# Attention in one streaming encoder layer: negated scores with a chained minimum, a fourth slot for turned weights, the output gate on GpSimd, stores on SyncE

## What is computed

```python
def dsa_attend(q, iq, iw, k, v, ik, q_pos, topk):
    ...                                             # sel: the topk keys that the indexer picks for a query
    logits = jnp.einsum('btgrd,btkgd->btgrk', qg, kg).astype(jnp.float32) * (A_HEAD_DIM ** -0.5)
    logits = logits - slopes[None, None, :, :, None] * dist[:, :, None, None, :]
    logits = jnp.where(valid[:, :, None, None, :], logits, -jnp.inf)
    prob = jax.nn.softmax(logits, axis=-1).astype(v.dtype)
    out = jnp.einsum('btgrk,btkgd->btgrd', prob, vg)
    return out.reshape(bsz, t, A_WIDTH)
# later: y_a = (o_a * silu(z_a)) @ w_branch_a
```

## Time and profile before

| | us |
|---|---|
| median of 3 runs | 3327.56 |
| lowest, highest | 3320.19, 3329.63 |
| the profiled execution, its time | 3322.89 |
| its span in the trace | 3321.2 |
| attention in the trace, first S to the store of the last tile | 1840.66 to 2523.75 |
| TensorE, VectorE, ScalarE, GpSimd busy in 1842 to 2525 | 559, 538, 402, 105 |

### The profile page before, as it was taken

One profiled execution on the slowest core, in us unless ns is written; L12 is line 12 of the kernel. 1 busy time (PEld: TensorE's weight loads), 2 busy tenths in 40 slices (PEclk: granted clock), 3 DMA queues, 4 the chain that ended last, 5 costly groups with the idle time before them and its releaser, 6 DMA issues.

```text
span 3321.2 us, 43027 instructions
## 1 busy us (share of the span) xinstructions
PE 2869.1 (86%) x14677; PEld 2570.8 (77%) x14677; DVE 2374.1 (71%) x4343; ACT 1601.6 (48%) x2638; POOL 1260.8 (38%) x875
## 2 busy tenths in 40 slices
PE   5899999999999989898642678888886999599998
PEld 4899999999999989898631455666665999488886
DVE  5378758629999999999346777878776646456564
ACT  3277477877776857656002555556653000211111
POOL 1000377777788768576040321111102333111120
PEclk9999999999999999999886899999998999799999
DMA  4333333333333223222483121111104455311210
GB/s 139 91 118 125 111 102 103 97 115 105 107 112 100 93 77 113 70 88 93 160 222 100 43 58 43 44 48 32 41 11 157 139 180 199 132 62 62 80 64 32
DMA packets 286182, 321.04 MB, mean 97 GB/s; under 512 B 37025, under 2 KB 258977, under 8 KB 282413
## 3 DMA queue, kind: packets, MB, share of 16 engines
q1 hardware_dynamic: 149037, 176.64, 17.7%
q10 hardware_dynamic: 135648, 137.80, 12.5%
q0 software_dynamic: 1312, 4.26, 0.4%
HBM read 194.46 MB, written 123.48 MB: 96 GB/s over the span
## 4 chain that ended last, share of the span: by engine, by line
PE 41%; DVE 36%; ACT 8%; issue 7%; DMA 4%; POOL 2%; ACTq 1%; SPq 0%; DVEq 0%; POOLq 0%
PE psum L2054 12%; DVE s_high L427 10%; PE psum L1177 10%; PE psum L1929 7%; DVE a_l L1760 4%; ACT s_ajunk L410 3%; DVE a_ptlo L1779 3%; PE psum L1663 2%; ACT v_product L820 2%; PE psum L1699 2%; DVE s_cand L429 2%; DVE s_g L428 1%; DVE s_high L459 1%; PE psum L1700 1%; PE psum L1157 1%
## 5 line engine op out<-in xcount | busy, mean ns | idle before, releaser
L1177 PE MATMUL psum<-hT_hi,j_whi 128*128 128x416 f32 x2440 | 870.8, 357 | 69.4 <-ACT j_out L1050 32.6
L1177 PE MATMUL psum<-hT_hi,j_wlo 128*128 128x416 f32 x2440 | 862.5, 353 | 0.0
L1177 PE MATMUL psum<-hT_lo,j_whi 128*128 128x416 f32 x2440 | 862.1, 353 | 0.0
L834 POOL TENSOR_TENSOR v_y<-v_y,v_product 128x422 f32<-128x422 f32 x580 | 712.9, 1265 | 256.2 <-ACT v_product L820 256.0
L1177 PEld LDWEIGHTS psum<-hT_hi,j_whi 128*128 128x128 f32 x2440 | 463.6, 190 | 87.7 <-ACT j_out L1050 39.1
L1177 PEld LDWEIGHTS psum<-hT_lo,j_whi 128*128 128x128 f32 x2440 | 464.7, 190 | 11.6
L1177 PEld LDWEIGHTS psum<-hT_hi,j_wlo 128*128 128x128 f32 x2440 | 463.6, 190 | 6.1
L427 DVE TENSOR_SCALAR_CACHE_REDUCE s_high<-s_key,s_cand 128x1024 int16<-128x1024 f32 (+4 forms) x240 | 392.9, 1637 | 8.4
L820 ACT ACTIVATE v_product<-v_x,v_taps 128x422 f32<-128x422 f32 x580 | 339.6, 640 | 74.7 <-POOL v_y L834 34.5
L1779 DVE TENSOR_TENSOR a_ptlo<-psum,a_pthi 128x512 fp32r<-128x512 f32 x338 | 228.2, 684 | 55.6 <-ACT a_pthi L1735 54.9
L1728 ACT ACTIVATE a_l<-a_l,a_nbias 128x512 f32<-128x512 f32 (+4 forms) x136 | 184.2, 1354 | 167.0 <-DVE a_nbias L1769 165.7
(11 more groups left out here) (286 smaller groups left out, 5401.3 us busy)
## 6 DMA issues: line engine op xcount, KB each, us to landing
T_dram<-j_out ACTq DMA_DIRECT2D x305, 208.0 KB, 1.9
j_w<-in_w_in ACTq DMA_DIRECT2D x59, 512.0 KB, 4.2
m_gate<-T_dram SPq DMA_DIRECT2D x60, 416.0 KB, 3.5
m_oraw<-B_dram SPq DMA_DIRECT2D x15, 832.0 KB, 6.5
SC_dram<-i_acc SPq DMA_DIRECT2D x40, 256.0 KB, 2.0
M_dram<-m_merged ACTq DMA_DIRECT2D x5, 1664.0 KB, 10.5
n_x<-in_x_prompt SPq DMA_DIRECT2D x16, 512.0 KB, 4.8
a_q<-T_dram SPq DMA_DIRECT2D x32, 256.0 KB, 6.6
```

The source lines that it names most:

```text
L834: pool.tensor_tensor(y[n % 2][:], y[n % 2][:], product[n % RING][:], ALU.add).then_inc(added, 1)
L1177: last = pe.matmul(bank, w[p][:, k, :], h[:, k, t0:t0 + SPAN], start=(k == 0 and q == 0), stop=(k == KD - 1 and q == 2))
```

## The change

The order of groups is the same; the program is written out tile by tile with constants. What differs:

- **Scores are negated**: the scale of the queries and of `nd` changes sign, R keeps the minimum, and takes as its start the minimum of the piece before (a value per partition, `lows[:, h, s-1:s]`), so the last piece holds the minimum of the head. E takes it as its bias, with scale -1. Before each R but a head's first, VectorE waits for its own R before it. L1768 and L1769 are gone.
- **A fourth slot** of turned weights takes the PSUM bank that the share had; the share now takes a turn in the ring, after W of the fourth last key tile. T runs up to 4 key tiles ahead: T of tile x+4 stands behind W of tile x, and T 2 and T 3 of a group stand before its first S.
- **The gate on GpSimd**: ScalarE copies the share to SBUF (`a_factor`, L1745 of the changed kernel) behind the last hi; GpSimd multiplies it by the gate (L1622), and later the added output by that (L1628). VectorE keeps the add alone.
- **Stores on SyncE**, each behind the loads of the tile two later.
- **Groups' ends** stand at x = 1 in place of x = 0.
- Loads of `nd` and of the gate wait for the last E and the last gate product, not for a tile's output.

```diff
-            pool.memset(scale[:, h:h + 1], HD ** -0.5 * 2.0 ** (h + 1)).then_inc(scale_set, 1)
+            pool.memset(scale[:, h:h + 1], -(HD ** -0.5) * 2.0 ** (h + 1)).then_inc(scale_set, 1)
...
-    QK, PT, PO, PB = 2, (2, 3, 4), (5, 6), 7
+    QK, PT, PO = 2, (2, 3, 4, 7), (5, 6)
...
-            if x == 0 and before:
+            if x == 1 and before:
                 e.finish(before)
...
+        def gate(group):
+            u, nu, _ = group.shares
+            pool.wait_ge(pt_free[u], nu + 1)
+            pool.wait_ge(za_full[group.p], group.m * 16 + 16)
+            pool.tensor_tensor(factor[group.g][:], factor[group.g][:], of_group(za, group), ALU.mult).then_inc(factor_made, 1)
+            pool.wait_ge(factor_made, group.n + 1)
+
+        def end(group):
+            o = of_group(oa, group)
+            pool.wait_ge(po_read[group.g], group.t + 1)
+            pool.tensor_tensor(o, o, factor[group.g][:], ALU.mult).then_inc(o_done[group.p], 1)
+
-        split(0, 0, 0)
-        with pool.Fori(0, DT // 2) as i:
-            split(i * 2 + 1, i, 1)
-            store(i * 2, i, 0)
-            split(i * 2 + 2, i + 1, 0)
-            store(i * 2 + 1, i, 1)
+        split(0)
+        split(1)
+        for group in groups:
+            if group.n:
+                end(groups[group.n - 1])
+            gate(group)
+            if group.g == 0 and 1 <= group.t < TILES - 1:
+                split(group.t + 1)
+        end(groups[-1])
...
+            if x + RING < tiles:
+                turn(group, x + RING)
+            if x + RING == tiles:
+                share(group)
+            if x + 2 >= tiles and following:
+                turn(following, x + 2 - tiles)
...
+            if s:
+                _, _, _, _, previous, uses, _ = group.units[(h - 4 * group.g) * len(pieces(group.keys)) + s - 1]
+                vec.wait_ge(qk_read[previous], uses + 1)
             vec.wait_ge(qk_full, n + 1)
-                                     scale=2.0 ** -(h + 1), scalar=LOWEST, op0=ALU.subtract, op1=ALU.max,
-                                     accum_out=peaks[:, h, s:s + 1]).then_inc(qk_read[b], 1)
-            if s == spans - 1:
-                vec.wait_ge(qk_read[b], nb + 1)
-                top = peaks[:, h, 0:1]
-                if spans > 1:
-                    top = peak[:, h:h + 1]
-                    do(vec.tensor_reduce(top, peaks[:, h, 0:spans], AX.X, ALU.max))
-                vec.tensor_scalar(nbias[:, h:h + 1], top, -1.0, None, ALU.mult).then_inc(head_ready, 1)
+                                     scale=2.0 ** -(h + 1), scalar=lows[:, h, s - 1:s] if s else HIGHEST, op0=ALU.add, op1=ALU.min,
+                                     accum_out=lows[:, h, s:s + 1]).then_inc(qk_read[b], 1)
```

More of the change, by code:

```diff
@@ L154 @@
     0, 1, 5, 6, 7, 9, 13, 17, 21, 25, 29, 33, 37)
[L157 to L165, removed]
 def doubled(eng, dst, src, sem):
@@ L1517, in stage_attend @@
[L1517 to L1555, removed]
+    class Group:
+        def __init__(self, n):
+            self.n, self.t, self.g = n, n // KVH, n % KVH
+            self.m, self.p, self.keys = self.t // 2, self.t % 2, keys_of(self.t)
+            self.heads = range(4 * self.g, 4 * self.g + 4)
@@ L1556, in together @@
+    def together(e, group, scored, before):
+        units, tiles = scored.units if scored else [], group.tiles if group else []
+        if group:
+            e.start(group, before is None)
         issued, heads = 0, []
-        for x in range(max(1, len(keys))):
-            if weighed:
-                e.turned(weighed, keys, x)
-            if x == 0 and before:
+        for x in range(max(1, len(tiles))):
+            if group:
+                e.turned(group, x)
+            if x == 1 and before:
@@ L1565, in together @@
             heads = [(h, at_x) for h, at_x in heads if at_x + 2 > x]
-            for unit in units[issued:-(-len(units) * 4 * (x + 1) // (3 * len(keys))) if weighed else None]:
+            for unit in units[issued:-(-len(units) * 4 * (x + 1) // (3 * len(tiles))) if group else None]:
                 e.unit(scored, unit)
@@ L1570, in together, with in_order @@
                     heads.append((unit[0], x))
-            if weighed:
-                e.weigh(weighed, keys, x, scored)
+            if group:
+                e.weigh(group, x, scored)
         for h, _ in heads:
             e.head(scored, h)
[L1575 to L1588, removed]
+    def in_order(e):
+        together(e, None, groups[0], None)
+        for n, group in enumerate(groups):
+            together(e, group, groups[n + 1] if n + 1 < len(groups) else None, groups[n - 1] if n else None)
+        e.finish(groups[-1])
     def by_head(slot):
@@ L1716, in tensor, with turn @@
-        group_order(Actions(start=start, turned=turned, unit=unit, weigh=weigh, all_weighed=all_weighed),
-                    lambda n: pe.Fori(0, n))
+        def turn(group, x):
+            kt, w, u, nu, nk, n, _ = group.tiles[x]
+            if x == 0:
+                pe.wait_ge(exp_done, HEADS * group.t + 4 * group.g + 4)
+            if nu:
+                pe.wait_ge(pt_free[u], nu)
+            for r, h in enumerate(group.heads):
+                last = pe.transpose(c.psum[0:w, PT[u], r * P:(r + 1) * P], L[h][:, kt * P:kt * P + w], c.ident[:])
+            last.then_inc(pt_full, 1)
@@ new lines, in share, with start @@
+        def share(group):
+            u, nu, n = group.shares
+            pe.wait_ge(rs_ready, group.n + 1)
+            pe.wait_ge(pt_free[u], nu)
+            for r, h in enumerate(group.heads):
+                last = pe.matmul(c.psum[:, PT[u], r * P:(r + 1) * P], rs[:, h:h + 1].to_broadcast([P, P]), c.ident[:],
+                                 start=True, stop=True)
+            last.then_inc(pt_full, 1)
+        def start(group, first):
+            if first:
+                turn(group, 0)
+                turn(group, 1)
+            turn(group, 2)
+            turn(group, 3)
@@ L1719, in scalar @@
+        in_order(Actions(start=start, unit=unit, weigh=weigh))
     def scalar(act):
@@ L1788, in finish @@
[L1788 to L1796 removed]
+            o = oa[group.p][:, 4 * group.g:4 * group.g + 4, :].rearrange("d h t -> d (h t)")
```

221 lines of the change are left out of this document (112 added, 109 removed).

## The result

| | before | changed |
|---|---|---|
| median of 4 runs, us | 3326.34 (3320.19 to 3329.63) | 3367.19 (3363.41 to 3368.96) |
| the profiled execution's span | 3321.2 | 3365.4 |
| attention in the trace, first S to the store of the last tile | 683.1 | 730.0 |
| TensorE, VectorE, ScalarE, GpSimd busy in attention | 559, 538, 402, 105 | 576, 473, 409, 179 |

The ratio is 1.0123, 95% interval 1.0106 to 1.0141: the changed kernel is slower by 41 us. The forecast was +24 (3347 us), with a range that reached to 3370; 3367 lies near the upper end of that range and 4 us above the forecast's own 3363. In the trace attention is 46.9 us longer, and what follows it takes 796 us in place of 797, so the whole difference lies in attention.

What follows compares the result with a forecast made beforehand. Attention was taken as bound by a loop between VectorE and TensorE, no engine full. Gains of -53, split waits +65 and low clock +12 sum to +24 us on 3322.9: 3347 us, range 3322 to 3370.

Steps and rivals of the forecast that it cites:

- What bounds it: Attention: no engine full; a loop between VectorE's R and lo and TensorE's T and W, period 5.38 us.
- GpSimd's order: GpSimd's query split queues behind the gate product; TensorE waits 3.4 to 5.4 us per tile 1 to 15, +65 us.
- The clock: TensorE in attention: eight waits of about 5 us each lower the granted clock, 1.5 us each, +12 us.
- rival C: TensorE: every wait for a split lowers the clock, the 3.4 us ones too; 3358 to 3386 us, 13%.
- Reduction and negation: VectorE's loop: L1768 and L1769 gone, R waits for R; gains 0.07 of 5.38 us, last E 0.3 sooner.
- Rival E: VectorE's R: the chained start value costs 154 ns each; +39 us, 3362 us; no separate chance, within the forecast's 63%.
- Share, gate, add: Group heads and ends: first R 1.35 us sooner in tiles 12 to 15; about 1.5 us for each of 34 groups.
- The fourth slot: Ring of turned weights: hides nothing more by itself, 0; costs one T of 0.44 us before a group's first S.
- Rival A: Attention loop: freed from TensorE's waits for lo, period falls from 5.38 to 4.6 us; 3288 us, 10%.
- Rival B: Attention: granted clock stays high through the waits and a group gains 1.8 us; +4, 3327 us, 12%.
- Rival D: GpSimd: the split is not late, so only the -53 us remains; 3270 us, 2%.

Runs made afterwards that it cites:

- early split: Changed kernel with GpSimd's split of the next tile's queries placed ahead of the gate product of the same group; 3293.06 us, 0.9915 of before.

## Why the prediction was right, and where its sum was off

*What bounds it, and GpSimd's order.* Right, wait by wait: 15 of them, 67.2 us against 65. In tiles 12 to 15 they are 5.06 (forecast 4.9), in 8 to 11 5.5 (5.4), in 4 to 7 3.22 (3.4), in 1 to 3 4.04 (3.4). The gate product took 1.27, above both ends given for it, which made 0.3 of each wait; with it the waits of tiles 4 to 7 should have been longer than forecast and were shorter, so a term of theirs was 0.5 too high, and which is not traced. (The forecast's 4.9 is 11.1 less 6.3, which is 4.8, and its 1.35 for the head is 8.61 less 7.2, which is 1.41: slips that change nothing.) The early split removes 69 us: 59 of waits, and their clock.

*The clock.* The size was too high and its spread wrong: 12 forecast, 5 to 9 measured, and the lower level came behind 14 of the 15 waits, those of 3.2 to 4.0 us too, at well under 1 us each, and not behind eight at 1.5. Shorter waits brought it as well: the 2.7 us of the early split, and before the change one of 1.46 us out of many such (at 2067.31; the granted clock was 0.67 in 2068 to 2072). So the two rows of gMLP did not bound the waits that lower the clock. That is the mechanism of rival C without its price. The Trainium skill (TensorE: Matmul & The Clock Gate, "HAM oscillation — how this bites in real kernels") has the rule that a wait which recurs ahead of each block of work makes every block start at the slow clock. The trace agrees with it for 14 of the 15 waits. The forecast let the first 3.4 us of work take up to twice as long; why they take so much less extra was not tested.

*Reduction and negation: this is the term that was mis-sized.* The loop was laid out right but for the pair. From a lo to the R behind the next W are 3.92 us in the changed kernel (2431.31 to 2429.72 + 5.51), forecast 3.96. The two R then take 1.59 to the lo, and not 1.35: 0.92 and 0.67, for 0.73 and 0.61 + 0.01. The 0.73 came from a small reduction that follows an R; an R that does so starts 0.92 behind. And the start value, taken at nothing, moved the spacing from 0.61 to 0.67. That is 0.20 us in a period of tiles 12 to 15. Tiles 0 to 3 have no such pair, and their 8 of the 84 periods do not pay it, so an estimate for the rest is 15 us; taking the chain out gave 17 to 19. Alone, on the version without the chain, the wait costs 20 us and the start value 11. Rival E had asked 15 for the second and nothing more for the first, which the forecast held at 0.13 x 84 = 11; its 3362 came closest to 3367.

The forecast fell 17 short of 41, and that is not this term alone. All but the split's order was to give 53 and gave 31, 22 less; the waits cost 67 and not 65; the clock cost 5 to 9 and not 12. That the clock was put too high hid a part of the error, by luck. The direction did not hang on it: 67 us of waits stood against 54 us gained at most, even without the chain.

*Share, gate, add.* The first R of a group stands 0.90 behind the first S (2417.28 to 2418.18), forecast 0.9, before 1.95. With the chain out, attention is 42.1 us shorter than before (the time 45.5, by the ratio) while 8.0 us of waits remain, so the edits and the saved negation make 50 to 54. The forecast's 53 is met there, but not as it was put together: it held 0.07 x 84 = 6 for the loop, which without the chain gives about 0.16 x 84 = 13, so heads and ends come to some 37 to 41 and not 47. Head, end and add were not run apart from each other.

*The fourth slot.* Nothing by itself: right in this order, and with three it was, if anything, slightly faster. Rival A was wrong for this change (5.51 is above 5.0), but its arithmetic was that of a real version: with T ahead of W the period is 4.78. Rival B's larger gain was not there. Rival D's 3270 was the time without the waits if the sum of the rest held; the early split's 3293, with 8 us of waits left, says how far it did not.

*Left open.* A group of tiles 12 to 15 takes 29.00; the forecast's 27.95 and four periods of 0.20 more make 28.75. The last 0.25 is not traced. Nor is it settled why four slots seem to cost 5 to 7 us over three, whether the order with T ahead of W needs the fourth, and how much of that order's gain belongs to the share, which moved with T.

## What to carry to other kernels

On an engine that takes its instructions in program order, as GpSimd did in these traces, an instruction that waits for something late holds up everything queued behind it; ask of each moved operation which finished work it now makes wait, and put first what has its inputs and is wanted elsewhere. Replacing a small operation by a dependence can cost more than the operation: a reduction of 156 ns per head was cheaper than 0.31 us between two neighbours and 0.06 for each start value, though against two small operations the same dependence still gained 8 us. A deeper buffer by itself gave nothing here; letting T past the wait, with that buffer, gave 32 us.

## What the runs showed of the hardware beyond what was expected

- An R that starts from a value per partition, and not from a constant, takes 728 ns in place of 687, and its successor starts 0.67 behind it in place of 0.61. The same with a column that never changes (208 of them).
- An R that waits for the accumulator of the R just before starts 0.91 to 0.92 behind it, against 0.61, in the changed kernel and with the wait alone: the accumulator is read out in an instruction of 0.08 at the end, and then 0.22 go by.
- GpSimd's product on 64x512 takes 1272 ns, and its operation on 128x1024, with twice the elements in each partition and twice the partitions, 1893. Half of that, 0.95, was too low a guess.
- A product of two operands in SBUF on VectorE took up to 2.72 us while GpSimd made its split, and 0.68 without. A lo and an add that read one operand from PSUM took 0.69 and 0.67 there, with GpSimd at work beside them.
- The length of a wait alone did not tell whether TensorE's clock falls to the lower level. It fell behind 14 of 15 waits of 3.2 to 5.5 us, behind all three of 2.7 us with the early split, and in the kernel that does matmuls ahead of the wait behind all four of 2.5 us but only two of the four of 2.1 us; before the change a wait of 2.53 us left it high and one of 1.46 us did not.
